# Two transformer stacks on one Trainium2 core: one opening stage, rotations inside the value stages, mixer tables split 8-4-4

## The chip, the core and the metric

The kernel runs on one core of one Trainium2 chip. The metric is the device time of one execution in microseconds (us). Everything is computed in 32-bit floats.

## What is computed

Two blocks follow each other on 512 latent tokens and 256 context tokens of width 1024. The first block has two layers, latent attention (MLA) and gated delta rule (GDN), each with a feed-forward part. The second has windowed attention with a sink and a state-space mixer (S5). Every layer is modulated by a shift, a scale and a gate, which are products of a condition vector with a large matrix. Cut to what the change touches:

```python
mod = silu(c) @ w_mod[i] + b_mod[i]              # 6 x 1024 for the latent tokens, the same with c_ctx for the context
h = x * (1 + scale) + shift
lat = h @ mla_w_in                               # 1024 -> 512 + 256 + 64
cq  = rms_norm(lat[..., :512], q_norm)
ckv = rms_norm(lat[..., 512:768], kv_norm)
k_rope = lat[..., 768:]
q = cq @ w_q_up; kv = ckv @ w_kv_up              # k and v of 8 heads
q_rope, k_rope = rotate(q_rope), rotate(k_rope)  # u1 * cos - u2 * sin, u2 * cos + u1 * sin; latent tokens only
...
abar = exp(lam * dt); bbar = (abar - 1) / lam * b   # S5, complex; the kernel builds tables from their powers
```

## The kernel before, in words

All data is feature-major: 128 features on the partitions, tokens along the free axis. `hu` holds the residual stream h and the modulated input u, both 8 tiles of 768 columns; `area` is a large scratch region; `tmp` and `stat` are small; `P` is the whole of PSUM, four pieces of two banks. `mod` holds the modulation, one column for each row of 128 features and condition.

The program is a sequence of blocks. In a block each engine has its own instruction stream, and a block ends when all engines have come to its end. A wait or a DMA that an engine still has to issue therefore holds everybody.

**Products.** `dense` (line 153) runs one matrix product as a block. The weights come through a ring of two slots: SP loads a slot when TensorE has counted a group in `mm_done` (`stream`, line 136), and prefetches the first two groups of the next product. TensorE does `per` output tiles of `kt` x 128 rows a group over 512 and 256 columns (line 187). In the trace each matmul in 32 bits is two instructions. ScalarE evicts, VectorE works on what was evicted. `dense_tokens` (line 236) does the same with tokens on the partitions, for the values of both attentions: v_up (4 groups, two k tiles) and att_v (2 groups, eight k tiles), six token tiles of 256 columns each.

**Modulation.** One row of `w_mod` (128 x 1024, 512 KB) is multiplied by a condition on VectorE and summed over its columns (`mod_product`, line 1933), twice for each row, as there are two conditions. `mod_stage` (line 1958) does a range of rows beside a `dense`: GpSimd loads them through four slots, VectorE multiplies. `ModStream` does two rows for each group of a `dense`, loaded by SP in the same queue as the weights (line 2001).

**The start**, in this order, each its own block: rows 0 to 15 of the modulation with the loads of x, ctx and constants (lines 2053 to 2092); `s5_prepare`, which computes the powers of the S5 poles in a chain of 32 dependent steps on VectorE with ScalarE's Exp and Sin in between, transposes them on TensorE, and stores three tables (`fa`, `pc`, `a8`) to DRAM, and waits until they have landed (lines 1383 to 1522); `modulate` (line 2115), all 16 passes of u on ScalarE; `dense("mla_in")`, seven output tiles, with rows 16 to 47; a copy; `normalise` for q and for kv (line 278); `dense("q_up")` with rows 48 to 51; a copy of the rotary key; `dense("k_up")`; `dense_tokens("v_up")`; `turn`; attention.

**Rotation.** `turn` (line 343) first loads a permutation and the cosine and sine tables, then for each block of 128 features: TensorE permutes the rows (line 360), VectorE multiplies the permuted block by sin (369) and the block by cos (370), and adds (373). 5 blocks for MLA, 20 for the second attention.

**Mixer tables.** `s5_tables` (line 1525) builds the sixteen S5 tables on GpSimd beside the feed-forward products: 0 to 8 beside ffn_in0, 9 to 13 beside ffn_out0, 14 and 15 beside ffn_in1. It reads `fa` and `pc`; its block can end only when the stores of its last table have landed. The feed-forward blocks ffn_in0 and ffn_in1 also carry a `ModStream` of 44 rows each.

## Time and profile before

| | |
|---|---|
| time, median of 3 runs | 5419.24 us (5417.52 to 5436.85) |
| the profiled execution, its own time | 5445.98 us |
| its span, first to last instruction | 5444.2 us |
| TensorE matmul busy | 4622.4 us, 85% of the span |
| VectorE busy | 1992.6 us, 37% |
| ScalarE busy | 950.8 us, 17% |
| GpSimd busy | 1230.8 us, 23% |
| mean granted TensorE clock | 0.895 |
| HBM | 96 GB/s over the span |

Engines in the rows: PE is TensorE's matmul, PEld its weight load, DVE is VectorE, ACT ScalarE, POOL GpSimd, SP SyncE; a q behind the name is the engine's sequencer, which issues DMAs. `L187` is line 187 of the kernel. A granted clock of 1.00 is 2.4 GHz, 0.50 is 1.2 GHz. Busy shares are means over some forty stages with different limits, so the stages have to be looked at one by one.

### The profile page before, as it was taken

Reading aid. Unit: us, or ns where it says so; the run is one execution under the profiler, and the core shown is the slowest. Engines: PE = TensorE matmul, PEld = TensorE weight load, DVE = VectorE, ACT = ScalarE, POOL = GpSimd, SP = SyncE. Lnnn points to the kernel's source line nnn. Section 1 sums busy time; section 2 is a strip of 40 time slices with the busy share of each in tenths; the row PEclk is TensorE's granted clock in tenths of the full one; section 3 lists DMA queues with packets and bytes.
Section 4 is the critical chain, followed back from the end, with each engine's and each line's share of the span. In section 5 each row is a group of like instructions: output and inputs, shape, how many; then the busy total and the mean of one; then the engine's idle time right before and its main releaser. Section 6 shows DMA issues by size and latency. Waiting matters only on the chain. (4 is left out here: it accounts for less than half of the span.)

```text
span 5444.2 us, 51256 instructions
## 1 busy us (share of the span) xinstructions
PE 4622.4 (85%) x18898; PEld 2798.7 (51%) x18898; DVE 1992.6 (37%) x3915; ACT 950.8 (17%) x2104; POOL 1230.8 (23%) x1460
## 2 busy tenths in 40 slices
PE   2789979998979855788898997986789978698998
PEld 1445545554535544677443443555555546594443
DVE  6613236550045566233107412018830017900001
ACT  1112220000021153343101001003420022010000
POOL 0000029998800048800006100001000000340000
PEclk9887889998989876787999998998999989757999
DMA  4310026764401025322216421110001144663211
GB/s 172 129 40 0 16 78 204 199 199 143 147 31 54 28 96 155 104 70 70 73 70 194 166 99 70 47 50 2 0 23 54 46 137 145 237 185 126 77 70 62
DMA packets 244735, 526.70 MB, mean 97 GB/s; under 512 B 140752, under 2 KB 147408, under 8 KB 214992
## 3 DMA queue, kind: packets, MB, share of 16 engines
q1 hardware_dynamic: 189856, 338.20, 19.0%
q0 software_dynamic: 54416, 185.89, 11.2%
q8 instruction: 104, 1.70, 0.1%
q14 instruction: 71, 0.58, 0.0%
q10 hardware_dynamic: 288, 0.32, 0.0%
HBM read 429.42 MB, written 94.77 MB: 96 GB/s over the span
## 5 line engine op out<-in xcount | busy, mean ns | idle before, releaser
L187 PE MATMUL P<-hu,ring 128*128 128x512 f32 (+1 forms) x4896 | 1741.3, 519 | 141.2 <-PEq L2103 60.2
L187 PEld LDWEIGHTS P<-hu,ring 128*128 128x128 f32 x4896 | 935.8, 191 | 946.5 <-issue 898.8
L187 PE MATMUL P<-area,ring 128*128 128x512 f32 (+1 forms) x3104 | 1165.3, 538 | 74.3 <-PEq L162 36.4
L187 PEld LDWEIGHTS P<-area,ring 128*128 128x128 f32 x3104 | 595.0, 192 | 643.8 <-issue 597.3
L2129 DVE SCALAR_TENSOR_TENSOR hu<-hu,tmp 128x512 f32 (+3 forms) x48 | 47.7, 1001 | 835.9 <-ACT tmp L2123 835.9
L1566 POOL TENSOR_TENSOR area<-area 128x512 f32<-128x512 f32 (+2 forms) x128 | 226.3, 1768 | 10.0
L1544 POOL DMA_DIRECT2D area<-s_fa x64 | 40.7, 635 | 790.0 <-POOLq L289 775.6
L449 PE MATMUL P<-area 128*128 (+3 forms) x480 | 185.8, 497 | 27.1 <-POOL area L431 27.1
L1933 DVE SCALAR_TENSOR_TENSOR area<-area 128x1024 f32<-128x1024 f32 x88 | 191.7, 2178 | 31.0 <-DMA area<-in_w_mod 29.5
L1565 POOL TENSOR_TENSOR area<-area 128x512 f32<-128x512 f32 (+2 forms) x128 | 203.0, 1586 | 0.0
L1564 POOL TENSOR_TENSOR area<-area 128x512 f32<-128x512 f32 (+2 forms) x128 | 193.9, 1515 | 38.2 <-DMA area<-in_s_bn 33.7
L2123 ACT ACTIVATE tmp<-P,mod 128x512 f32<-128x512 f32 x72 | 41.3, 615 | 851.5 <-PE P L187 851.5
L1755 PE MATMUL P<-hu,ring 128*128 128x256 f32 (+1 forms) x512 | 168.2, 492 | 24.9 <-PEq L103 24.9
L2152 DVE TENSOR_TENSOR area<-tmp 128x768 f32<-128x768 f32 (+1 forms) x44 | 66.1, 1501 | 314.1 <-ACT tmp L2136 314.1
L2136 ACT ACTIVATE tmp<-P 128x768 f32<-128x768 f32 (+1 forms) x88 | 57.1, 701 | 691.0 <-PE P L187 691.0
L2165 DVE TENSOR_TENSOR area<-area,tmp 128x512 f32 (+3 forms) x48 | 35.3, 778 | 373.7 <-ACT tmp L2161 373.7
L1933 DVE SCALAR_TENSOR_TENSOR area<-stat,area 128x1024 f32<-128x1024 f32 x88 | 163.8, 1861 | 11.1 <-DMA stat<-in_w_mod 5.2
L1712 POOL DMA_DIRECT2D area<-s_b x16 | 8.5, 530 | 694.0 <-POOLq L103 461.0
L472 PE MATMUL P<-tmp,area 128*128 128x128 f32 x1152 | 158.6, 282 | 0.2
L2312 DVE TENSOR_TENSOR area<-area,tmp 128x512 f32 (+1 forms) x16 | 11.1, 692 | 392.8 <-ACT tmp L2309 392.8
L369 DVE TENSOR_TENSOR tmp<-P,area 128x512 f32<-128x512 f32 x25 | 17.1, 684 | 355.6 <-PE P L360 355.6
L1970 POOL DMA_DIRECT2D tmp<-in_w_mod x30 | 15.9, 532 | 579.1 <-POOLq L2103 483.9
(306 smaller groups left out, 5618.8 us busy)
## 6 DMA issues: line engine op xcount, KB each, us to landing
ring<-in_w_ffn_in SPq DMA_DIRECT2D x44, 1024.0 KB, 5.9
ring<-s_c POOLq DMA_DIRECT2D x32, 1152.0 KB, 6.3
area<-in_w_mod SPq DMA_DIRECT2D x52, 512.0 KB, 3.6
stat<-in_w_mod SPq DMA_DIRECT2D x44, 512.0 KB, 3.6
ring<-in_w_ffn_out SPq DMA_DIRECT2D x16, 1408.0 KB, 6.2
s_c<-area POOLq DMA_DIRECT2D x32, 576.0 KB, 3.6
area<-s_fa POOLq DMA_DIRECT2D x64, 256.0 KB, 7.6
area<-in_s_bn POOLq DMA_DIRECT2D x64, 256.0 KB, 8.0
```

The source lines that it names most:

```text
L187: last = nc.tensor.matmul(c.P[:, 2 * s + j, a:b], c.ring[:, slot, (j * kt + k) * 128:(j * kt + k + 1) * 128], x[:, k, a:b], start=k == 0, ...
L449: last = nc.tensor.matmul(S[n % 2][:, a:b], qs[:, j, t * 128:t * 128 + 128], k(i, j, key, key + b - a), start=True, stop=rope is None)
L472: last = nc.tensor.matmul(O[n % 2], vs[:, j, key, :], probT[:, n % 2, b * 128:b * 128 + 128], start=b == 0, stop=b == len(tiles) - 1)
L1564: tt(out, re_, a, ALU.mult)
L1565: step(tt(tmp, im_, b, ALU.mult))
L1566: step(tt(out, out, tmp, ALU.add if sign > 0 else ALU.subtract))
L1755: last = nc.tensor.matmul(c.P[:, 2 * (g % 2) + j, a:b], c.ring[:, s, (j * KD + k) * 128:(j * KD + k + 1) * 128], c.u[:, k, a:b], start=k = ...
L1933: return c.nc.vector.scalar_tensor_tensor(out=junk, in0=weights, scalar=1.0, in1=c.view(CONDS, 2, D)[:, cc % 2, :], op0=ALU.mult, op1=ALU. ...
L2123: last = act_fn(tmp[:, a:b], ps[:, a:b], ACT.Copy, scale=c.mod[:, bass.ds(g * per + (j + gate), 1), cc:cc + 1].rearrange("p a b -> p (a b)"))
L2129: return vec_fn.scalar_tensor_tensor(out=hk, in0=hk, scalar=ALPHA, in1=tmp[:, 0:w].unsqueeze(1), op0=ALU.mult, op1=ALU.add)
L2136: return act_fn(tmp[:, 0:w], ps[:, 0:w], ACT.Silu if j == 0 else ACT.Copy)
L2152: return vec_fn.tensor_tensor(hidden[:, one(g), 0:w], pairs_first[0][:, 0:w].unsqueeze(1), tmp[:, 0:w].unsqueeze(1), ALU.mult)
```

## The change

One block, `opening`, takes the place of the modulation of rows 0 to 15, `s5_prepare`, `modulate`, `dense("mla_in")`, the copy and both norms. SP and GpSimd load modulation rows and x and ctx tile by tile. VectorE makes the four products of one k and adds the bias, ScalarE makes tile k of u, and TensorE multiplies it with the weights of the first four output tiles, which are all loaded before and accumulate in the four pieces of PSUM. Tiles 4 to 6 follow, then sums of squares, transposes. VectorE does the chain of the powers when the modulation is done, and the scalings by the norms last; the root is Ln and Exp instead of Sqrt and reciprocal. The tables are stored without a wait; the wait stands at the end of SP's stream in q_up (`settle`).

Rows 16 to 35 of the modulation move to q_up, 36 to 43 to k_up, 44 to 51 to a `ModStream` in mla_out, which also loads and activates the conditions; ffn_in0 then does not. The rotary key is evicted straight to its place, so the copy block behind q_up goes. The rotations become part of `dense_tokens`: TensorE permutes between value tiles and, where blocks are left, behind them; GpSimd multiplies by cos, VectorE by sin and adds. The mixer tables are split 8, 4 and 4.

```diff
@@ program @@
-    s5_prepare(c)
-    modulate(modulated(0))
...
-    early = mod_stage(c, "mla_in", 16, 48, mod_slots, flat_stat[:, 0:D])
-    dense(c, "mla_in", u, BOTH, copy_to(lat, per=1), pool=early[0], vector=early[1])
...
-    normalise(c, "q_rms", lat, 4, T, BOTH, 1e-6, vcol("mla_q_norm"))
-    normalise(c, "kv_rms", lat[:, 4:6, :], 2, T, BOTH, 1e-6, vcol("mla_kv_norm"))
...
-    late = mod_stage(c, "q_up", 48, 52, mod_slots, flat_stat[:, 0:D])
+    opening(c, lat, q_all[:, 0, :])
+    early = mod_stage(c, "q_up", 16, 36, mod_slots, flat_stat[:, 0:D])
     dense(c, "q_up", lat, BOTH, lambda g, j, ps, tmp: act_fn(q_all[:, one(g * 2 + (j + 1)), :], ps[:, 0:T].unsqueeze(1), ACT.Copy),
-          pool=late[0], vector=late[1])
-    with nc.Block() as block:
...
-            act_fn(q_all[:, 0, :], k_hold, ACT.Copy)
-    dense(c, "k_up", lat[:, 4:6, :], BOTH, copy_to(k_nope))
-    dense_tokens(c, "v_up", lat[:, 4:6, :], 256, v_tok)
-    turn(c, "mla_rope", q_all, 5, area(13 * T, 3, 512), ("mla_trig", "mla_perm"))
+          pool=early[0], vector=early[1], settle=lambda sp: sp.wait_ge(c.s5_stored, 48))
+    late = mod_stage(c, "k_up", 36, 44, mod_slots, flat_stat[:, 0:D])
+    dense(c, "k_up", lat[:, 4:6, :], BOTH, copy_to(k_nope), pool=late[0], vector=late[1])
+    dense_tokens(c, "v_up", lat[:, 4:6, :], 256, v_tok, (q_all, 5, area(13 * T, 3, 512), ("mla_trig", "mla_perm")))
...
-    residual("mla_out", q_all[:, 5:13, :], 16, (0, 1), BOTH)
+    residual("mla_out", q_all[:, 5:13, :], 16, (0, 1), BOTH, mods=ModStream(c, "mla_out", 44, 4, fresh=0))
...
-                 (lambda pool: s5_tables(c, pool, KF * T, 0, 9), lambda pool: s5_tables(c, pool, KF * T, 9, 14)),
-                 mods=ModStream(c, "ffn_in0", 52, KF, fresh=0))
+                 (lambda pool: s5_tables(c, pool, KF * T, 0, 8), lambda pool: s5_tables(c, pool, KF * T, 8, 12)),
+                 mods=ModStream(c, "ffn_in0", 52, KF))
...
-    feed_forward(1, (0,), LATS, hidden, (lambda pool: s5_tables(c, pool, KF * T, 14, 16), None),
+    feed_forward(1, (0,), LATS, hidden, (lambda pool: s5_tables(c, pool, KF * T, 12, 16), None),
...
-    dense_tokens(c, "att_v", u, 256, v2)
-    turn(c, "att_rope", qk, 20, area(24 * T, 3, 512), ("att_trig", "att_perm"))
+    dense_tokens(c, "att_v", u, 256, v2, (qk, 20, area(24 * T, 3, 512), ("att_trig", "att_perm")))
@@ dense_tokens @@
+    per = blocks // groups
         @block.sync
         def _(sp):
-            stream(c, sp, name, ahead)
+            sp.dma_start(perm, c.ins[tabs[1]]).then_inc(landed, 16)
+            sp.dma_start(tables[:, 0:2, :].rearrange("p a b -> p (a b)"), c.ins[tabs[0]]).then_inc(landed, 16)
+            stream(c, sp, name)
         @block.tensor
+            def partners(n):
+                if n >= 2:
+                    pe.wait_ge(turned, n - 1)
+                nc.tensor.matmul(spare[n % 2], perm, y[:, n, 0:LAT], start=True, stop=True).then_inc(partner, 1)
+            pe.wait_ge(landed, 32)
+            for g in range(groups):
...
                 for t in range(T // 128):
+                    if t % 2 == 0 or per > 3:
+                        if n < blocks and n < (g + 1) * (per + 1):
+                            partners(n)
+                            n += 1
...
+            while n < blocks:
+                partners(n)
+                n += 1
+        @block.gpsimd
+            for n in range(blocks):
+                pool.wait_ge(partner, n + 1)
+                nc.gpsimd.tensor_tensor(y[:, n, 0:LAT], y[:, n, 0:LAT], cos, ALU.mult).then_inc(kept, 1)
+        @block.vector
+            for n in range(blocks):
+                dve.wait_ge(partner, n + 1)
+                if n >= 2:
+                    dve.wait_ge(done, n - 1)
+                nc.vector.tensor_tensor(c.tmp[:, n % 2, 0, 0:LAT], spare[n % 2], sin, ALU.mult).then_inc(turned, 1)
+                dve.wait_ge(turned, n + 1)
+                dve.wait_ge(kept, n + 1)
+                nc.vector.tensor_tensor(y[:, n, 0:LAT], y[:, n, 0:LAT], c.tmp[:, n % 2, 0, 0:LAT], ALU.add).then_inc(done, 1)
@@ new: opening @@
+        @block.sync
+            sp.dma_start(flat(conds), ins["conds"][0:1, :].broadcast_to([128, 2 * D])).then_inc(conds_in, 16)
+            sp.dma_start(first_w[0], ins["w_mod"][0]).then_inc(mod_in[0], 16)
+            sp.dma_start(h[:, 0, 0:LAT], x[:, 0, :]).then_inc(x_in[0], 16)
+            for n in range(0, 4, 2):
+                sp.dma_start(weights[n], ins["w_mla_in"][n]).then_inc(w_in[n], 16)
+            for k in range(1, KD):
+                sp.dma_start(first_w[k], ins["w_mod"][k]).then_inc(mod_in[k], 16)
+                sp.dma_start(h[:, k, 0:LAT], x[:, k, :]).then_inc(x_in[k], 16)
...
+            sp.wait_ge(mm, 4)
+            c.load_slot(sp, "q_up", 0, c.first["q_up"] % 2)
+            c.load_slot(sp, "q_up", 1, (c.first["q_up"] + 1) % 2)
+            sp.wait_ge(turned_k, 4)
+            sp.dma_start(c.s5["fa"].rearrange("r t x y -> x (r t) y"), turned).then_inc(stored, 16)
+            sp.wait_ge(dv, 32)
+            sp.dma_start(c.s5["pc"].rearrange("b p x -> p b x"), pcs).then_inc(stored, 16)
+            sp.dma_start(c.s5["a8"], a8.rearrange("p a b c d -> p (a b c d)")).then_inc(stored, 16)
+        @block.gpsimd
+            for k in range(KD):
+                pool.dma_start(first_w[8 + k], ins["w_mod"][8 + k]).then_inc(mod_in[8 + k], 16)
+                pool.dma_start(h[:, k, LAT:T], x[:, k, :]).then_inc(ctx_in[k], 16)
+                if k == 0:
+                    for n in range(1, 4, 2):
+                        pool.dma_start(weights[n], ins["w_mla_in"][n]).then_inc(w_in[n], 16)
+            nc.gpsimd.memset(eps, 1e-6).then_inc(based, 1)
...
+        @block.tensor
+            for n in range(4):
+                pe.wait_ge(w_in[n], 16)
+            for k in range(KD):
+                pe.wait_ge(shifted, k + 1)
+                for j in range(4):
+                    for a, b in BOTH:
+                        last = mmul(c.P[:, j, a:b], weights[j][:, 128 * k:128 * k + 128], u[:, k, a:b], start=k == 0, stop=k == KD - 1)
...
+            tile(4)
+            pe.wait_ge(consts, 32)
+            pe.wait_ge(kept, 4)
+            sums(range(4), c.P[:, 3, :])
+            tile(5)
+            tile(6)
+            pe.wait_ge(kept, 5)
+            sums(range(4, 6), c.P[:, 0, :])
+            pe.wait_ge(dv, 28)
+            pe.wait_ge(kept, 6)
+            for n in range(4):
+                if n >= 2:
+                    pe.wait_ge(turned_k, n - 1)
+                for m in range(4 * n, 4 * n + 4):
+                    last = nc.tensor.transpose(c.P[:, 1, 512 * (n % 2) + 128 * (m % 4):512 * (n % 2) + 128 * (m % 4) + 128],
+                                               fsel[:, m // 2, m % 2, :], c.ident[:, :])
+        @block.scalar
+            act_fn(flat(conds), flat(conds), ACT.Silu).then_inc(silu_c, 1)
+            for k in range(KD):
+                act.wait_ge(added, k + 1)
...
+                for cc, (a, b) in enumerate(((0, LAT), (LAT, T))):
+                    last = act_fn(u[:, k, a:b], h[:, k, a:b], ACT.Identity, scale=c.mod[:, 8 + k, cc:cc + 1], bias=c.mod[:, k, cc:cc + 1])
...
+            for n in range(4):
+                keep(n)
+            for n in range(4):
+                square(n)
+            act.wait_ge(dv, 14)
+            act_fn(flat(fs), flat(ph), ACT.Sin, scale=TURN)
+            act_fn(flat(fc), flat(fc), ACT.Sin, scale=TURN).then_inc(ac, 1)
+            keep(4)
+            keep(5)
+            square(4)
+            square(5)
+            keep(6)
+            act.wait_ge(based, 3)
+            root(0, c.P[:, 3, :], 512)
+            root(1, c.P[:, 0, :], 256)
+            for n in range(4):
+                act.wait_ge(pe_done, n + 1)
+                act_fn(flat(turned[:, 4 * n:4 * n + 4, :]), c.P[:, 1, 512 * (n % 2):512 * (n % 2) + 512], ACT.Copy).then_inc(turned_k, 1)
+        @block.vector
+            for k in range(KD):
+                for n in (k, 8 + k):
+                    dve.wait_ge(mod_in[n], 16)
+                    for cc in range(2):
+                        if count:
+                            dve.wait_ge(made, count)
+                        mod_product(c, n, cc, first_w[n], junk).then_inc(made, 1)
+                        count += 1
+                if k == 0:
+                    dve.wait_ge(based, 3)
+                dve.wait_ge(made, count)
+                V.tensor_tensor(pair(k), pair(k), base.rearrange("p (a k) -> p a k", a=2)[:, :, k].unsqueeze(2).broadcast_to([128, 2, 2]),
+                                ALU.add).then_inc(added, 1)
...
+            dve.wait_ge(added, KD)
+            dve.wait_ge(ac, 1)
+            step_(tt(grow, re, step, ALU.mult))
...
+            scaled(range(4), 0, "mla_q_norm")
+            scaled(range(4, 6), 1, "mla_kv_norm")
```

## Rows read from the trace of the kernel before

**Rows 1.** Windows of the stages up to q_up, columns by the heading.
```profile
core 0: us, PE busy (x) PEld busy (x) DVE busy (x) ACT busy (x) POOL busy (x), PEclk, DMA share, GB/s
0.00:52.70 52.70, 0.00 (x0) 0.00 (x0) 39.82 (x66) 3.19 (x2) 5.53 (x13) 1.00 0.70 266
52.70:98.90 46.20, 3.68 (x16) 3.27 (x16) 30.46 (x67) 9.38 (x18) 0.00 (x0) 0.92 0.20 61
98.90:108.90 10.00, 0.00 (x0) 0.03 (x1) 0.00 (x0) 9.68 (x16) 0.00 (x0) 0.50 0.00 0
108.90:184.50 75.60, 75.51 (x224) 43.52 (x224) 66.59 (x108) 4.92 (x7) 15.91 (x30) 0.96 0.72 247
184.50:198.50 14.00, 0.00 (x0) 0.00 (x0) 12.74 (x22) 0.76 (x1) 1.06 (x2) 0.58 0.35 131
198.50:235.60 37.10, 11.52 (x24) 5.96 (x24) 20.85 (x13) 7.81 (x9) 0.00 (x0) 0.64 0.00 0
235.60:300.80 65.20, 64.96 (x192) 37.48 (x192) 10.03 (x17) 7.59 (x11) 2.10 (x4) 0.96 0.20 69
```
**Rows 2.** Timeline of the first stage: start us, us, engine, line, operation.
```profile
6.40 17.71 SPq L2060 DMA_DIRECT2D ones<-in_ones  x1
9.83 1.23 DVE L1933 SCALAR_TENSOR_TENSOR stat<-area 128x1024 f32<-128x1024 f32 x1 [9.83 <-DMA area<-in_w_mod]
```
**Rows 3.** Groups of VectorE's instructions by line, 0 to 53 us.
```profile
L1933 DVE SCALAR_TENSOR_TENSOR stat<-area 128x1024 f32<-128x1024 f32 x32 | 39.2, 1225 | 12.4 <-DMA area<-in_w_mod 9.8 <-DVE stat L1933 0.5
```
**Rows 4.** Window of the DMA in the first stage.
```profile
10.00:15.00 5.00, 0.00 (x0) 0.00 (x0) 4.76 (x8) 0.00 (x0) 0.00 (x0) 1.00 1.03 417
```
**Rows 5.** Window of TensorE's clock at mla_in's start.
```profile
109.00:115.00 6.00, 6.00 (x7) 2.38 (x8) 1.25 (x3) 0.00 (x0) 2.11 (x4) 0.50 0.72 235
```
**Rows 6.** Timeline of the mixer powers: first step, transposes, last copy, last store.
```profile
55.55 0.29 DVE L1450 TENSOR_TENSOR area<-area 128x128 f32<-128x128 f32 x1 [3.21 <-ACT area L1425]
...
84.05 3.68 PE L1521 MATMUL P<-ident,area 128*128 128x128 f32 x16 [84.05 <-DVE area L1497]
...
87.76 0.60 ACT L1435 ACTIVATE area<-P 128x512 f32<-128x512 f32 x1 [0.26 <-PE P L1521]
...
90.46 3.70 SPq L1419 DMA_DIRECT2D s_a<-area  x1
```
**Rows 7.** Timeline of both value stages and their rotations.
```profile
329.34 20.96 PE L257 MATMUL P<-ring,area 128*128 128x256 f32 x96 [1.86 <-PEq L162]
...
352.43 0.43 SPq L352 DMA_DIRECT2D area<-in_mla_perm  x1
356.82 6.50 PE L360 MATMUL P<-area 128*128 128x512 f32 x10 [6.51 <-DMA area<-in_mla_perm]
...
368.38 0.69 DVE L373 TENSOR_TENSOR area<-area,tmp 128x512 f32<-128x512 f32 x1
...
3601.05 41.68 PE L257 MATMUL P<-ring,hu 128*128 128x256 f32 x192 [1.97 <-PEq L162]
...
3691.06 0.69 DVE L373 TENSOR_TENSOR area<-area,tmp 128x512 f32<-128x512 f32 x1
```
**Rows 8.** Windows behind ffn_in0 and ffn_out0, and of ffn_in1 with tables beside it.
```profile
1229.10:1252.80 23.70, 0.01 (x1) 0.00 (x0) 8.28 (x4) 1.51 (x2) 14.25 (x14) 0.54 0.39 141
1482.90:1491.50 8.60, 0.03 (x2) 0.05 (x1) 0.96 (x1) 1.05 (x2) 0.00 (x0) 0.75 0.43 152
2878.60:2991.50 112.90, 111.72 (x255) 49.23 (x256) 82.59 (x71) 10.74 (x16) 91.86 (x66) 0.98 0.77 228
```
**Rows 9.** Timeline of GpSimd: tables' first and last DMA in ffn_in0, two products.
```profile
772.86 0.63 POOL L1544 DMA_DIRECT2D area<-s_fa  x1 [202.76 <-POOLq L289]
...
1244.08 0.60 POOL L1601 DMA_DIRECT2D s_fb<-area  x1 [0.30 <-POOL area L1566]
...
1261.70 1.26 POOL L1564 TENSOR_TENSOR area<-area 128x512 f32<-128x512 f32 x1 [4.34 <-DMA area<-in_s_bn]
...
2986.24 2.13 POOL L1564 TENSOR_TENSOR area<-area 128x512 f32<-128x512 f32 x1
```

More of the change, by code:

```diff
@@ L55 @@
 PRODUCTS = [
-    ("mla_in", 8, 1), ("q_up", 4, 2), ("k_up", 2, 2), ("v_up", 2, 2), ("mla_out", 8, 2),
+    ("q_up", 4, 2), ("k_up", 2, 2), ("v_up", 2, 2), ("mla_out", 8, 2),
     ("ffn_in0", 8, 2), ("ffn_out0", KF, 1),
@@ L165, in _ @@
             stream(c, sp, name, more=mods and mods.load)
+            if settle:
+                settle(sp)
         if pool:
@@ L233, in _, with dense_tokens @@
                 vector(eng)
-def dense_tokens(c, name, x, width, out, ahead=True):
+def dense_tokens(c, name, x, width, out, turn):
     nc = c.nc
@@ L240, in dense_tokens @@
     at, groups = c.first[name], c.ins["w_" + name].shape[0]
-    copied = c.sem(name + "_copied")
+    copied, landed, partner, turned, kept, done = (c.sem(f"{name}_{n}") for n in ("copied", "landed", "partner", "turned", "kept", "turn_done"))
     psum = c.P[:, :, :].rearrange("p a b -> p (a b)")
+    y, blocks, tables, tabs = turn
+    cos, sin, perm = tables[:, 0, :], tables[:, 1, :], tables[:, 2, 0:128]
+    spare = [psum[:, 1536:2048], psum[:, 3584:4096]]
+    per = blocks // groups
     with nc.Block() as block:
```

415 lines of the change are left out of this document (191 added, 224 removed).

## The prediction

> **What bounds the kernel now.** I read the windows by stage first, because the change reshapes a few stages out of some forty and the rest keeps its length. Up to 108.9 us TensorE does nothing but 16 transposes: 52.7 us of modulation products on VectorE, 46.2 us of mixer powers with their stores, 10.0 us in which ScalarE alone modulates. Then mla_in holds TensorE for 75.6 us, 14.0 us pass in which VectorE finishes 64 modulation products, and the two norms take 37.1 us with TensorE busy in 11.5 of them. q_up's first matmul starts at 235.6 us [rows 1]. The reader should see that the engines take turns: before q_up the work that only TensorE can do (75.5 us of mla_in and 11.5 us of sums) is little over a third of the time. Two more places are serial: each rotation stands behind its value stage [rows 7], and in ffn_in0 GpSimd, which builds 9 of 16 mixer tables there, is done 15 us after TensorE, so that TensorE idles 23.7 us; at the end of ffn_out0 a tail of the same kind makes 8.6 us [rows 8, 9].
>
> **The opening.** VectorE starts its first product at 9.83 us, when modulation row 0 has landed [rows 2]; 32 products took 39.2 us busy at 1225 ns [rows 3], and from 9.83 to 52.7 about 1.31 us each with the read-out and the wait. The four products of a pair k take 5.2 us; the new add after each pair I take at 0.3 us, so 5.5 us a pair. DMA: before VectorE can start k=1, some 5.7 MB must land (condition rows 1, rows 0 and 8 together 1, rows 1 and 9 together 1, x and ctx of k=0 0.4, four weight tiles 2, vectors 0.3); at 417 GB/s [rows 4] from about 3 us on that is 17 us, against 15.3 when VectorE is free. I charge 1.7 us, once: a later pair needs 1.4 MB, 3.3 us, less than VectorE's 5.5. VectorE ends at 17 + 7 x 5.5 = 55.5, say 56; ScalarE's pair of passes (9.68 us for eight pairs [rows 1], 1.2 each) ends the last tile at 57.5.
>
> TensorE works beside this. Seven tiles of mla_in took 75.5 us [rows 1]; the first 6.0 us, after an idle stretch, ran at a granted clock of 0.50, 1.2 GHz [rows 5], which costs 3 us; so 10.35 us a tile. Four tiles for one k are an eighth of four, 5.2 us, against 5.5 us between tiles of u, so TensorE follows VectorE: it starts at 17, has made up the slow start by the third k, and ends k=7 at 62.7. Then, in its program's order: tile 4 (73), four sums of squares (5.2, to 78.2), tiles 5 and 6 (to 99), two sums (to 101.5). ScalarE's squares lie inside tile 4. The powers' chain runs on VectorE beside it: 55.55 to 84.05 before [rows 6], now from 59 plus some 3 us for the sines that queue behind ScalarE's squares, to about 91. It is hidden with 10 us to spare; if it came that much later it would show one for one. Behind the last sum comes what is exposed: two Ln and Exp pairs, and 16 transposes with four copies that took 3.7 us before (84.05 to 87.76 [rows 6]), together to about 109. ScalarE does them in order, so the copies stand behind the roots. VectorE's six scalings (0.9 us each, 1225 ns scaled to 768 columns) are over by then. SP issues the stores of the tables behind the last copy; their issue alone took from 88.4, when the last copy was done, to 94.16, the third blocked for 3.70 us [rows 6]: 5.8 us, and an engine that issues holds the stage open. End 115. The landing wait (until 98.9 before) moves to q_up's end, where it is long over. q_up starts at 115 instead of 235.6: **-120.6 us**.
>
> Unknowns of the opening. ScalarE's two roots may need one load of its function tables or several: I give this 3 us down and 4 up, between 112 and 119. GpSimd issues 18 DMAs before it makes the base of the sums for which VectorE waits at k=0; at about 0.55 us each this ends at 11 us, free. If GpSimd's queue blocked as SP's did, whose eleventh issue took 17.71 us [rows 2], VectorE would stand until about 24: up to +10 us. I take zero, since the nearest rows of GpSimd's own queue, the eight loads and ctx, show no such wait.
>
> **Products moved.** 32 rows leave mla_in. q_up takes 20: 40 x 1.31 + 4.4 to the first landing + 0.7 = 57.5 us, under its 65.2 [rows 1]; if the stores delay the loads by 5 us it still fits. k_up takes 8: 16 x 1.31 + 5.1 = 26.1 us, which passes its 20.7 us of warm matmul, so VectorE ends that stage; since the copy block ahead of it goes (1.2 us) and the stage had lasted 25.6, from q_up's end to v_up's start comes **-0.5 us**. mla_out takes 8 beside 82 us of matmul, with the conditions' DMA and Silu ahead of ScalarE's first eviction, which is due after 20 us: +0.2 us for a last small add. ffn_in0 loses its reload of the conditions, which hid.
>
> **v_up and its rotation.** Before: 329.3 to 369.1 [rows 7]. Now TensorE waits first for the tables, which SP can only issue at the stage's start: 4.8 us by the same pair of DMAs (the second issue at 352.43, the first 0.4 before it, the partner matmul at 356.82). TensorE then is cold, 3 us. 21.0 of values, five partner products of 0.86: 4.3. Last copy 1.5. End 329.3 + 34.7: **-5 us**.
>
> **att_v and its rotation.** Before: 3601.05 to 3691.7 [rows 7], of which 40 us are 20 turns of 2.0 us. Now 5 + 3 + 41.7 + 12 partners (10.3) bring it to 3661; eight turns are left behind the values. VectorE's share of a turn falls from three passes of 0.6 to two, 1.4 us with the dependence. But GpSimd's product takes 1.26 us alone [rows 9], and beside VectorE's two-input work 2.13 [rows 9]. If the two exclude each other in the add, a turn is 1.26 + 0.69 = 2.0 us, no shorter than before; if not, 1.4. I take 2.0, by the row with both at work: 16 us, plus 1.5, to 3678.7: **-13 us** (at 1.4: -18; at 2.8: -7).
>
> The Trainium skill, "SBUF — State Buffer", section "Who interferes with whom", says that a VectorE instruction with two SBUF inputs and a GpSimd instruction that reads SBUF block each other for a whole instruction. By it the turn is 2.0 us and the move of the cosine product to GpSimd buys nothing in the tail. The trace agrees as far as it goes: products of 1.23 us on VectorE stretch beside the tables (82.6 us busy in 112.9 [rows 8]).
>
> **Tables.** GpSimd took 471 us for 9, from 772.86 to 1244.1 [rows 9]: 52.4 each. Eight end at 1192, before TensorE's end at 1229; what then ends ffn_in0 is ScalarE's eviction, VectorE's product and three small adds, about 3.6 us: 23.7 - 3.6 = **-20.1 us**. In ffn_out0, four instead of five end 50 us early; 8.6 us become about 4.2, an eviction of two ScalarE passes, VectorE's residual and the change of blocks, an estimate from the 3.6 above: **-4.4 us**. In ffn_in1 four instead of two: with GpSimd at work 1.2 us of TensorE were lost in 112.9 [rows 8]; I take as much again: **+1.2 us**. Four end after 260 of 306 us.
>
> **Sum.** -120.6 - 0.5 - 5 + 0.2 - 13 - 20.1 - 4.4 + 1.2 = -162. The profiled execution took 5445.98 us, 27 above the median of the runs shown. Against itself it would be 5284; taken off the median, 5419 - 162 = **5257 us**.
>
> **Rivals.** (1) *The forecast*, chance 0.72: 5235 to 5280.
> (2) *TensorE stays at 1.2 GHz while it is fed tile by tile.* A k then takes 10.3 us, eight take 82, and the phase ends at 99 instead of 62.7: +37, or with GpSimd's blocked queue +10: 5267 to 5304. For it: TensorE waits before each k, and after gaps of some us it runs slow [rows 5]. Against: at half clock it is behind VectorE and so never idle, which is how it got its clock back in 6 us in mla_in. Chance 0.14.
> (3) *More is won*: turns of 1.4 us, warm starts, stores issued faster: 5235 and below, down to 5228. Chance 0.08.
> (4) *The change doesn't pay in its side parts*: rotations bring nothing, ffn_in0 is held by its two-condition products. Only the opening: 5419 - 121 = 5298. Chance 0.04.
> (5) *Slower than before.* In ffn_in1 SP loads each weight slot behind the wait for the modulation products of the group before. If four tables lock VectorE so that four products and the silu product take more than TensorE's 14 us a group (111.7 us for eight [rows 8]), every group waits. To lose the 162 us over 22 groups a group would have to take 21 us; at 27 (products of 6 us, five times their 1225 ns) it is 22 x 13 = +286, less the 162: 5543. For it: VectorE's work per group is already 10 us there, not 6. Against: TensorE idled for 1.2 us in those eight groups. Chance 0.02.
>
> **How the numbers follow.** The range 5230 to 5302 takes in (1), (2) and most of (4); what it leaves out is the far end of (3), (5), and the 19 us by which the runs of before differ. About 0.5%, 27 us, is what a measurement of this kernel can tell from no change. Faster by more: 0.96, all of (1) to (4) but 0.02 kept for something unseen that eats the gain, which is the chance of no change; slower: 0.02, (5).
>
> **What would show it.** q_up's first matmul near 115 us; matmuls of the opening from 17 us, granted clock 1.00 from about 23; k_up ended by VectorE; TensorE of both value stages starting 5 us late; eight turns of 2.0 us behind att_v; ffn_in0's gap 3 to 4 us; GpSimd over by 3150 in ffn_in1. Wrong if q_up starts after 130, if TensorE in ffn_in1 idles over 5 us, or if stages that the change doesn't touch change by over 10 us in sum.

## The result and the profile after

The changed kernel takes **5267.31 us** (median of 4 runs, 5254.79 to 5272.83) against 5418.38 us for the kernel before beside it (4 runs, 5412.9 to 5436.85): ratio 0.97, interval 0.968 to 0.9719, 151 us less, inside the range 5230 to 5302. Its profiled execution took 5272.83 us with a span of 5271.1, and is 5.5 above its median; that of before was 27 above its own, so between the two traces lie 173 us.

The page of the changed kernel: busy time by engine, and TensorE's busy tenths and granted clock in 40 slices of 132 us:

```profile
PE 4601.1 (87%) x18898; PEld 2791.0 (53%) x18898; DVE 1979.2 (38%) x3891; ACT 954.4 (18%) x2108; POOL 1274.8 (24%) x1489
...
PE   7899799999799656888989997977799788798998
...
PEclk9878899999899766888999998999999999658999
```

TensorE's busy tenths before, in slices of 136 us, were

```profile
PE   2789979998979855788898997986789978698998
```

The first digits are what changed: TensorE is busy for seven tenths of the first slice instead of two. The windows of the opening stages, after (columns as in [rows 1]):

```profile
core 0: us, PE busy (x) PEld busy (x) DVE busy (x) ACT busy (x) POOL busy (x), PEclk, DMA share, GB/s
0.00:17.50 17.50, 0.00 (x0) 0.00 (x0) 5.09 (x9) 4.50 (x4) 11.60 (x25) 1.00 0.88 340
17.50:63.10 45.60, 44.95 (x128) 25.22 (x129) 38.50 (x80) 13.97 (x28) 0.00 (x0) 1.00 0.62 239
63.10:101.90 38.80, 38.80 (x122) 22.82 (x122) 27.14 (x51) 13.27 (x17) 0.00 (x0) 1.00 0.08 28
101.90:118.60 16.70, 2.94 (x18) 2.33 (x16) 5.75 (x6) 9.18 (x11) 0.00 (x0) 0.61 0.32 95
118.60:184.70 66.10, 64.14 (x193) 37.19 (x193) 49.70 (x82) 9.07 (x12) 10.66 (x20) 0.97 0.64 214
184.70:210.50 25.80, 20.86 (x64) 12.03 (x64) 20.08 (x34) 6.04 (x8) 4.21 (x8) 0.95 0.59 205
210.50:245.90 35.40, 26.90 (x106) 20.93 (x106) 6.92 (x10) 5.81 (x4) 8.76 (x9) 0.89 0.29 92
```

TensorE waits for its first data until 17.5 us, then is full for 84.4 us in two windows, with VectorE and ScalarE at work beside it, and idles again for most of the 16.7 us ahead of q_up. What stood one behind the other in [rows 1] now lies side by side. The stages, from each one's first matmul to the next one's, in the two traces:

```
                             before   after    difference   forecast
start to q_up                 235.6    118.6     -117.0      -120.6
q_up, k_up, v_up with turns   136.2    127.3       -8.9        -5.5
MLA attention                 263.0    261.6       -1.4         0
mla_out                        87.0     87.3       +0.3        +0.2
ffn_in0                       480.4    460.5      -19.9       -20.1
ffn_out0                      238.6    232.5       -6.1        -4.4
norm behind it                 53.5     48.6       -4.9         0
delta-rule heads              681.2    677.7       -3.5         0
ffn_in1                       309.1    307.7       -1.4        +1.2
att_qk and att_v              304.0    288.5      -15.5       -13
second attention              306.1    309.6       +3.5         0
```

The rows with a forecast and the norm make -173 (forecast -162); all stages that no edit touches make less than 1 us in sum in this pair of traces, though single ones move by 3.5.

### The profile page after: what moved, and what is told of

Read it like the earlier page. It is cut to its first block and busy times, and to the rows that moved or that the text cites. A ratio compares the mean times of both kernels' runs of the same rounds, so it can differ in the third digit from the quotient of the medians.

```text
span 5271.1 us, 51177 instructions
## 1 busy us (share of the span) xinstructions
PE 4601.1 (87%) x18898; PEld 2791.0 (53%) x18898; DVE 1979.2 (38%) x3891; ACT 954.4 (18%) x2108; POOL 1274.8 (24%) x1489
## 5 line engine op out<-in xcount | busy, mean ns | idle before, releaser
L189 PE MATMUL P<-hu,ring 128*128 128x512 f32 (+1 forms) x4672 | 1665.9, 520 | 118.7 <-PEq L333 40.1
L189 PEld LDWEIGHTS P<-hu,ring 128*128 128x128 f32 x4672 | 892.4, 191 | 892.0 <-issue 849.2
L1802 DVE SCALAR_TENSOR_TENSOR area<-stat,area 128x1024 f32<-128x1024 f32 x96 | 207.1, 2157 | 8.0 <-DMA stat<-in_w_mod 1.7
L1624 PE MATMUL P<-hu,ring 128*128 128x256 f32 (+1 forms) x512 | 168.3, 492 | 24.9 <-PEq L103 24.9
L1624 PEld LDWEIGHTS P<-hu,ring 128*128 128x128 f32 x512 | 98.1, 192 | 94.8 <-issue 88.1
L483 PEld LDWEIGHTS P<-tmp,area 128*128 128x128 f32 x1152 | 144.7, 197 | 1.9 <-ACT tmp L518 1.7
```

What stands on the lines that cost most here:

```text
L189: last = nc.tensor.matmul(c.P[:, 2 * s + j, a:b], c.ring[:, slot, (j * kt + k) * 128:(j * kt + k + 1) * 128], x[:, k, a:b], start=k == 0, ...
L483: last = nc.tensor.matmul(O[n % 2], vs[:, j, key, :], probT[:, n % 2, b * 128:b * 128 + 128], start=b == 0, stop=b == len(tiles) - 1)
L1624: last = nc.tensor.matmul(c.P[:, 2 * (g % 2) + j, a:b], c.ring[:, s, (j * KD + k) * 128:(j * KD + k + 1) * 128], c.u[:, k, a:b], start=k = ...
L1802: return c.nc.vector.scalar_tensor_tensor(out=junk, in0=weights, scalar=1.0, in1=c.view(CONDS, 2, D)[:, cc % 2, :], op0=ALU.mult, op1=ALU. ...
```

## The experiments

**The base again.** After all others the changed kernel was timed once more, beside the last two versions.

> The changed kernel unaltered, beside the two others on the same chip and with the same runs of before, so that their difference from it can be read: 5255 to 5273, as before. Stages that no edit touches (MLA attention, the delta-rule heads, the second attention) will again lie several us apart from those of its first trace; the opening, ffn_in0, ffn_out0 and att_v will not (within 0.6 us).

Measured: 5251.25 us (5236.21 to 5254.81), ratio 0.9677 (0.9653 to 0.9701), 172 us under the 5423.25 of before; so it lay a few us under the interval that I gave. MLA attention 250.7 instead of 261.6, heads 667.7 instead of 677.7, ffn_in0 460.7, ffn_out0 232.7, att_v 72.9, q_up at 117.98 instead of 118.60. The same program did the same work in other time. In the stages of the table above that the edits touch, and the norm, this second trace is 172.8 us under the one of before (the first 173.2); in all other stages together it is 23.9 under it, where the first was 0.1 above. The windows from 440 to 480 us, inside MLA attention, first the changed kernel's first trace:

```profile
440.00:480.00 40.00, 37.17 (x132) 19.08 (x131) 11.26 (x31) 9.00 (x19) 3.91 (x5) 0.74 0.00 0
```

and the second:

```profile
440.00:480.00 40.00, 37.17 (x165) 20.25 (x163) 14.72 (x39) 11.09 (x24) 3.91 (x5) 1.00 0.00 0
```

TensorE is busy for 37.17 of 40 us in both, at a granted clock of 0.74 and of 1.00, and gets through 132 and 165 matmuls. Over the whole of MLA attention TensorE is idle for 9.3 us in both traces and busy for 252.3 and 241.4, at granted clocks of 0.80 and 0.84: the 10.9 us are the clock's. So a part worth under 10 us can't be told from a total; below, each part is read in its own stage and the total only bounds it.

**The tables split 9-5-2 again**, all else as in the changed kernel (lines cut):

```
-  s5_tables(c, pool, KF * T, 0, 8), ... s5_tables(c, pool, KF * T, 8, 12)
+  s5_tables(c, pool, KF * T, 0, 9), ... s5_tables(c, pool, KF * T, 9, 14)
-  s5_tables(c, pool, KF * T, 12, 16)
+  s5_tables(c, pool, KF * T, 14, 16)
```

> The changed kernel with the mixer tables split 9-5-2 again. My theory: GpSimd outlasts TensorE in ffn_in0 and ffn_out0 and nothing else depends on the split. Then the gap behind ffn_in0 is some 24 us instead of 3.7, the gap behind ffn_out0 some 8 us instead of 2.6, and TensorE comes cold to the sums of the norm behind it (13.5 and 12.3 us instead of 10.6 and 10.6): +30 us, about 5297. ffn_in1 stays at 305 us of TensorE. Rival A, the gaps alone, clock untouched: +25. Rival B, two more tables beside ffn_in1 cost TensorE time there: ffn_in1 gets 2 us or more shorter when they go, and the sum is under +25.

Measured: 5284.31 us (5280.22 to 5286.1), ratio 0.9736 (0.9692 to 0.978): 17 above the changed kernel's first median and 33 above its second. By stage +20.6 in ffn_in0, +6.5 in ffn_out0, +4.5 in the norm behind it: 31.6, as my theory had it. In the totals of the two traces MLA attention, which ran 10.9 us shorter in this one, hides a third of that. TensorE's timeline of this kernel at ffn_out0's start and at the two halves of the norm's sums:

```profile
1114.63 6.08 PE L189 MATMUL P<-area,ring 128*128 128x512 f32 x7 [24.04 <-PEq L162]
...
1353.64 13.36 PE L339 MATMUL P<-hu,ones 128*128 128x512 f32 x32 [8.90 <-PEq L162]
1368.93 12.28 PE L344 MATMUL P<-tmp,ones 128*128 128x512 f32 x32 [1.93 <-ACT tmp L354]
```

and the changed kernel's:

```profile
1107.06 229.94 PE L189 MATMUL P<-area,ring 128*128 128x512 f32 x704 [3.67 <-PEq L162]
...
1339.60 10.56 PE L339 MATMUL P<-hu,ones 128*128 128x512 f32 x32 [2.61 <-PEq L162]
1352.09 10.59 PE L344 MATMUL P<-tmp,ones 128*128 128x512 f32 x32 [1.93 <-ACT tmp L354]
```

The gaps fall from 24.04 to 3.67 and from 8.90 to 2.61. The same 64 matmuls behind the second gap take 25.6 us after 8.90 us of idleness, at granted clocks of 0.79 and 0.86 in the two halves, and 21.2 us after 2.61, at 1.00 in both: behind the shorter gap TensorE kept its clock. ffn_in1, which has two tables here and four in the changed kernel, takes 307.6 here and 307.7 there: four cost nothing.

**The rotations behind their stages again** (the loop over blocks in a stage of its own, as before; all else as changed):

```
-    dense_tokens(c, "att_v", u, 256, v2, (qk, 20, area(24 * T, 3, 512), ("att_trig", "att_perm")))
+    dense_tokens(c, "att_v", u, 256, v2)
+    turn(c, "att_rope", qk, 20, area(24 * T, 3, 512), ("att_trig", "att_perm"))
```

> The changed kernel with the value stages and the rotations as separate blocks again, as in the kernel before. My theory: the traces' differences of 6.7 us (v_up) and 15 us (att_v) are the rotations' own: +22 us, about 5289. Rival, the value stages' cold start and the wait for the tables eat most of it: +10 or less.

Measured: 5282.74 us (5272.73 to 5299.82), ratio 0.9735 (0.9685 to 0.9785). att_qk and att_v together 303.4 instead of 288.5, +14.9; MLA attention starts 136.3 us behind q_up's first matmul (255.73 less 119.40) instead of 127.3, +9.0. In sum +23.9, against my +22; the rival (+10 or less) is out. As in the kernel before, VectorE does the cosine product here too; the next run shows that this adds nothing.

**The cosine product on VectorE** instead of GpSimd:

```
+                nc.vector.tensor_tensor(y[:, n, 0:LAT], y[:, n, 0:LAT], cos, ALU.mult).then_inc(kept, 1)
-        @block.gpsimd
...
-                nc.gpsimd.tensor_tensor(y[:, n, 0:LAT], y[:, n, 0:LAT], cos, ALU.mult).then_inc(kept, 1)
```

> The changed kernel with the product by cos on VectorE instead of GpSimd, inside the same stages. My theory (GpSimd's product and VectorE's add exclude each other, 1.27 + 0.69 us): the eight turns behind att_v take 2.0 us each either way, so the stage's length changes by under 1 us and the time stays within 3 us. Rival, the move to GpSimd takes work off the path: a turn gets 0.6 us longer, 5 us in the tail.

Measured: 5263.43 us (5226.44 to 5272.03), ratio 0.9679 (0.9621 to 0.9737); att_v 72.7 instead of 72.8. A turn in this kernel's tail, timeline:

```profile
3503.08 0.68 DVE L303 TENSOR_TENSOR tmp<-P,area 128x512 f32<-128x512 f32 x1
3503.68 0.68 DVE L304 TENSOR_TENSOR area<-area 128x512 f32<-128x512 f32 x1
...
3504.47 0.69 DVE L307 TENSOR_TENSOR area<-area,tmp 128x512 f32<-128x512 f32 x1
3505.07 0.68 DVE L303 TENSOR_TENSOR tmp<-P,area 128x512 f32<-128x512 f32 x1
```

and three turns of the changed kernel's:

```profile
3497.91 4.17 POOL L302 TENSOR_TENSOR area<-area 128x512 f32<-128x512 f32 x3 [3.04 <-PE P L265]
3499.29 1.67 DVE L314 TENSOR_TENSOR area<-area,tmp 128x512 f32<-128x512 f32 x1 [0.73 <-POOL area L302]
3500.88 0.68 DVE L311 TENSOR_TENSOR tmp<-P,area 128x512 f32<-128x512 f32 x1
3501.59 1.04 DVE L314 TENSOR_TENSOR area<-area,tmp 128x512 f32<-128x512 f32 x1
```

Three passes on VectorE come to 1.99 us a turn (3503.08 to 3505.07). With the cosine on GpSimd VectorE has two, but its add (L314, both inputs in SBUF) takes 1.67 and 1.04 us instead of 0.69 while GpSimd multiplies, and GpSimd's three products 4.17 instead of 3 x 1.27; the product that reads PSUM (L311) keeps its 0.68. Eight such turns end no sooner than eight on VectorE alone (17.0 us from the tail's first product to its last add with GpSimd, 17.1 without). The Trainium skill, "SBUF — State Buffer", section "Who interferes with whom", has this rule: a VectorE instruction with two SBUF inputs and a GpSimd one that reads SBUF exclude each other, one with a single SBUF input, outside its 2-port performance modes, does not. The trace agrees on both halves, and the run shows what follows: this part of the change is worth 0.

**Only the side parts**: the kernel before with the fused rotations and the split 8-4-4, without the new opening (against the kernel before, shortened; att_v is changed as v_up is).

```
-    dense_tokens(c, "v_up", lat[:, 4:6, :], 256, v_tok)
-    turn(c, "mla_rope", q_all, 5, area(13 * T, 3, 512), ("mla_trig", "mla_perm"))
+    dense_tokens(c, "v_up", lat[:, 4:6, :], 256, v_tok, (q_all, 5, area(13 * T, 3, 512), ("mla_trig", "mla_perm")))
...
-  0, 9 and 9, 14 and 14, 16
+  0, 8 and 8, 12 and 12, 16
```

> The kernel before with only the rotations inside the value stages and the tables split 8-4-4; the opening is the old one. My theory, the parts add up: v_up 6.7, att_v 15, behind ffn_in0 19.9, behind ffn_out0 6.1, warm norm 4.8, together -52 us, about 5366, and so 100 to 120 us for the opening. Rival, the parts depend on each other (the modulation of rows 44 to 51 in mla_out shortens something in ffn_in0, the opening's gain is larger alone): the sum is off by 10 us or more.

Measured: 5369.21 us (5358.47 to 5377.42), ratio 0.9895 (0.9848 to 0.9943): 50 us of gain against 5419.22, and q_up still at 235.61. By stage its trace gives 53.4 in the stages touched, where I had expected 52. With the opening's 117.0 that makes 170.4 of the 173.2 by which these stages shrank in the changed kernel: the parts add up. The opening was not run alone; its 117 are the difference that is left.

**The two roots in the order Ln, Ln, Exp, Exp:**

```
-            root(0, c.P[:, 3, :], 512)
-            root(1, c.P[:, 0, :], 256)
+            log(0, c.P[:, 3, :], 512)
+            log(1, c.P[:, 0, :], 256)
+            root(0)
+            root(1)
```

> The two roots of the opening in the order Ln, Ln, Exp, Exp instead of Ln, Exp, Ln, Exp; nothing else. Theory: each change between the two functions loads a table for 1.28 us, four of them between 100.28 and 108.15, and these lie on the path (copies of the transposes, last store, q_up). Two loads go (2 x 1.28), the last root ends at about 106.4 instead of 108.99, the stores are issued 2.5 us earlier, and q_up's first product starts at about 116.1 instead of 118.60. Rival: the last transposes or the powers' stores set the end anyway (those stores are issued from 112.60 because of the queue, not of the copies): q_up stays at 118 or later. In the total -2.5 us at most, which three rounds can't tell; it is read from the trace.

In the changed kernel ScalarE's timeline from the last sums of squares to the copies of the transposes reads:

```profile
100.28 1.28 ACT L2078 ACT_TABLE_LOAD   x1
...
102.49 1.28 ACT L2080 ACT_TABLE_LOAD   x1
...
104.65 1.28 ACT L2078 ACT_TABLE_LOAD   x1
...
106.86 1.28 ACT L2080 ACT_TABLE_LOAD   x1
108.15 0.84 ACT L2080 ACTIVATE hu<-hu 128x768 f32<-128x768 f32 x1
108.90 1.07 ACT L2098 ACTIVATE area<-P 128x512 f32<-128x512 f32 x2
```

and with the roots paired:

```profile
100.22 1.28 ACT L2078 ACT_TABLE_LOAD   x1
101.52 1.69 ACT L2078 ACTIVATE hu<-P,area 128x768 f32<-128x768 f32 x2
...
103.23 1.28 ACT L2083 ACT_TABLE_LOAD   x1
104.52 1.58 ACT L2083 ACTIVATE hu<-hu 128x768 f32<-128x768 f32 x2
```

Two loads for four, and q_up's first matmul at 115.53 instead of 118.60, 3.1 us earlier: two loads of 1.28 us and some overlap of like operations. Total 5257.9 us (5241.64 to 5265.76), ratio 0.97 (0.9653 to 0.9747), not to be told from the changed kernel's, as expected.

**The stores waited for in the opening:**

```
             sp.dma_start(c.s5["a8"], a8.rearrange("p a b c d -> p (a b c d)")).then_inc(stored, 16)
+            sp.wait_ge(stored, 48)
```

> Inside the opening stage SyncE waits for the three mixer stores before the stage ends, instead of leaving the wait to the end of q_up. Theory: the last store lands some 2 to 4 us behind its issue (114.45 to 118.15), and this goes on the path in full: q_up's first product at about 122 to 123 instead of 118.60, so moving the wait is worth 4 to 5 us, and the total is 4 us longer, inside what runs can tell. Rival: the stores have landed by the time that the issue queue lets SyncE go (its 3.70 us of issue is itself the wait for room), then q_up starts within 1.5 us of 118.60. The modulation loads in q_up no longer queue behind the stores: their first product comes nearer to the stage's start than the 6.9 us of the changed kernel.

Measured: q_up's first matmul at 122.09, and as the opening's tile 4 began 0.64 us earlier here (62.49 against 63.13), the wait costs 4.1 us. This part of the change is worth that. It has a small price: with the stores still under way the first modulation product of q_up starts 6.9 us behind q_up's first matmul (125.48 less 118.60), here 4.25 (126.34 less 122.09); q_up hides both. Total 5249.89 us (5242.77 to 5259.1), ratio 0.9693 (0.965 to 0.9737).

**The rotation tables issued in the stage before**, first at that stage's end (settle), then at its head:

```
-            sp.dma_start(perm, ...) and sp.dma_start(tables, ...)        in v_up and att_v
+    dense(c, "att_qk", ..., settle=turn_tables(c, *att_tabs, att_in))    e_tables_early
+    dense(c, "att_qk", ..., head=turn_tables(c, *att_tabs, att_in))      e_tables_first
```

> The rotation tables of both value stages are issued by SyncE at the end of the stage before (k_up, att_qk) and not at the start of the value stage. Theory: the first product of each value stage waits for SyncE's two table issues and the weights behind them (v_up's at 214.82 and att_v's at 3442.87 with 9.26 and 6.61 us idle before them). With the tables gone from the queue's head both start about 4 to 5 us earlier and TensorE stays at full clock, so that the stages end 5 to 7 us earlier each: v_up through to MLA attention 245.92 to about 240, att_v stage 72.8 to about 67; total -10 to -13 us. Rival: the stage start itself (barrier, semaphores, first weight tile over DMA) is the wait, and the tables lie beside it: less than 2 us each, total within 4 us of the changed kernel.

Measured: 5252.78 us (5248.39 to 5256.48), ratio 0.969 (0.9648 to 0.9733), and by stage almost nothing: att_v 73.0, MLA attention at 245.72. SyncE's and TensorE's timeline at att_v tells why:

```profile
3423.83 0.34 SPq L120 DMA_DIRECT2D ring<-in_w_att_v  x1
...
3424.21 0.44 SPq L317 DMA_DIRECT2D area<-in_att_perm  x1
3424.69 0.43 SPq L318 DMA_DIRECT2D area<-in_att_trig  x1
3430.22 2.07 PE L263 MATMUL P<-area 128*128 128x512 f32 x2 [6.42 <-DMA area<-in_att_trig]
```

In att_qk the last weight load waits for room in the ring until the last group is done, and the tables stand behind it in SyncE's program, so that att_v had them as late as before, and this run tests neither theory there. In k_up they were issued at 208.12 instead of 210.54, and v_up's first product came at 213.21 instead of 214.82; v_up then took 1.4 us longer, for a reason that I did not find. At the head of the stage, with SyncE's and TensorE's rows at the same place:

> The rotation tables of both value stages are issued as SyncE's first two instructions of the stage before (k_up, att_qk), ahead of the weights that wait for room in the ring; in the run before this one they stood behind those weights, were issued only as that stage ended, and the first product of att_v waited for them still (6.42 us, ended by the tables' DMA). Theory: the tables' transfer is the wait, and its place ahead of the blocked issues takes it away. att_v's first product waits about 2 us, as k_up's does (1.96 us behind the stage before), instead of 6.61, and TensorE keeps the full clock, so that the first 4 rotation and value products take half as long too: att_v 72.8 to 66 to 68 us. v_up's first product comes at 211.5 to 212.5 instead of 214.82 and gains 1 to 3 us, because TensorE has waited there for VectorE's last modulation products already and starts at the low clock either way. Total -6 to -9 us against the changed kernel, inside what the medians tell; it is read by stage. Rival: the stage's start (barrier and first weights) is the wait, then att_v stays above 71 us.

```profile
3380.67 20.98 SPq L120 DMA_DIRECT2D ring<-in_w_att_v  x2
3403.39 1.10 PE L265 MATMUL P<-area 128*128 128x512 f32 x2 [2.12 <-PEq L162]
```

att_v's first product now waits 2.12 us instead of 6.61 and runs at full clock, 1.10 us for the pair instead of 2.08. att_qk is 4.4 us shorter (211.0 against 215.4; the wait counts there) and att_v 2.7 (70.3 against 72.9). v_up's first product comes at 211.89 instead of 214.82 and MLA attention starts at 243.92, 2.0 earlier. In sum 9 us; the total, 5233.61 us (5227.17 to 5258.25), ratio 0.9658 (0.9631 to 0.9686), is 18 under the changed kernel beside it. Its trace is 22 under that kernel's, of which the heads, 9.4 us shorter with no edit in them, are chance.

**The opening with tile 6 last**, behind the transposes and both sums, with the stores and the second root beside it (TensorE's part of the edit; ScalarE's program follows it, with the first root beside tile 5):

```
             tile(5)
-            tile(6)
...
+            pe.wait_ge(dv, 28)
+            turns(0, 2)
             pe.wait_ge(kept, 5)
             sums(range(4, 6), c.P[:, 0, :])
...
+            turns(2, 4)
+            pe.wait_ge(kept, 6)
+            tile(6)
```

> The opening in another order: TensorE makes tile 6 (the rotary key) last, behind the sums of squares and the transposes, so that both roots with their four table loads, the copies and the stores run on ScalarE, VectorE and the queues beside tile 6's 32 products. Nothing is left out. Theory: the 19.35 us between TensorE's last product of the changed kernel's opening (99.25) and q_up's first (118.60) is a chain of ScalarE, transposes and issues that needs no TensorE; beside tile 6 (about 10.5 us) most of it is hidden: q_up's first product at 106 to 108 instead of 118.60, total -10 to -12 us. Rival: the stores of the mixer tables are late by the powers' chain on VectorE (last at 91.85) and SyncE's issues (112.16 to 118.15), so that the end moves by less than 5 us; or the waits put on TensorE ahead of tile 6 cost it its clock and tile 6 takes 21 us instead of 10.5, and q_up starts at about 117.

Measured: 5235.17 us (5230.78 to 5244.67), ratio 0.9666 (0.9623 to 0.971). Its timeline from the last transposes to q_up:

```profile
92.90 10.49 PE L2015 MATMUL P<-hu,tmp 128*128 128x512 f32 x32
...
93.77 0.39 SPq L1977 DMA_DIRECT2D s_fa<-area  x1
94.21 1.82 SPq L1979 DMA_DIRECT2D s_pc<-area  x1
...
95.98 1.28 ACT L2084 ACT_TABLE_LOAD   x1
96.07 3.68 SPq L1980 DMA_DIRECT2D s_a<-area  x1
...
104.54 35.71 PE L189 MATMUL P<-area,ring 128*128 128x512 f32 x109 [1.15 <-PEq L1957]
```

The stores with their 3.68 us of issue, the second root and its tables stand inside tile 6's 10.49 us, in which the granted clock is 1.00, and q_up follows 1.15 us behind it instead of 7.09. It starts at 104.54: 14.1 us earlier, 1.5 beyond the expected 106.

**Both together:**

> The opening with tile 6 last and the rotation tables issued first, together. Theory: both act in stages apart and add up: q_up's first product at 104.5 as with the opening's order alone, MLA attention about 15 to 17 us earlier than in the changed kernel's 245.92 (229 to 231), att_v about 5 us shorter; total 18 to 22 us below the changed kernel: about 5240 by the medians of earlier runs, ratio to before 0.965 to 0.967. Rival: with q_up earlier the modulation products in q_up and k_up become the bound (they run beside it on VectorE and waited for loads), and half of the opening's gain is given back: MLA attention at 238 or later.

Measured: **5226.4 us** (5206.35 to 5234.82, 5 runs), ratio 0.9632 (0.9609 to 0.9654). Its slowest run is below the fastest of the changed kernel beside it (5236.21), and the medians lie 24.9 apart. The stages touched give the same: MLA attention starts at 228.23 instead of 246.22, and att_qk with att_v takes 282.0 instead of 288.4, 24.4 in sum. The rival (MLA attention at 238 or later) is out. In one point I was off: q_up began at 105.80 and not at 104.5. Here TensorE was done with the first tile of u earlier, idled for 1.96 us (0.60 in the changed kernel) and then lost its clock for a few products, as the window behind that gap shows:

```profile
26.10:30.00 3.90, 3.88 (x8) 2.11 (x9) 3.73 (x8) 0.03 (x1) 0.00 (x0) 0.64 1.03 394
```

The 112 products behind it took 38.08 us instead of 36.76. This version beats both kernels.

## Why the prediction was right, point by point

**The likeliest case came.** The forecast's steps gave -162 and the two traces give -173 in the same stages. The second timing of the changed kernel gave -172, the first -151; the forecast lies between. How near the first median came is luck in part. By stage the sum was 11 us short, 3.6 too much for the opening and 14.6 too little for the rest, and the stages that no edit touches, which I had put at nothing, lie between 0.1 us above and 36.9 below those of before over the twelve later traces. My sign of being wrong, over 10 us of change in those stages, is no test for the same reason: two traces of one program give 0.1 and -23.9.

**The opening** was 3.6 us too short. Its first half held by two errors that cancel: VectorE waited for pair k=1 until 19.83 and not 17, as its timeline shows,

```profile
19.83 1.23 DVE L1802 SCALAR_TENSOR_TENSOR stat<-area 128x1024 f32<-128x1024 f32 x1 [4.29 <-DMA area<-in_w_mod]
```

but a pair then took 5.23 us, not 5.5, so that the last add ended at 56.3, where I had 56. The windows (340 GB/s over 17.5 us, then 397) have 6.9 MB moved by 19.83, where I had counted 5.7: about 1.2 MB that this pair did not need had come with it. Which, no run tried. TensorE started at 17.55 and ended the last k at 63.1, where I had 62.7. The second half is where the term was mis-sized. The "two Ln and Exp pairs, and 16 transposes with four copies ... together to about 109" ended at 112.14. From 101.5 to 109 they had 7.5 us, of which the four passes of the roots (0.90, 0.84, 0.90, 0.84) and the transposes and copies (3.7) fill 7.2, so there was room for none of ScalarE's four table loads of 1.28 us; with two of them gone q_up started at 115.53. The stores' issue took 6.0 us (112.16 to 118.15), where I had 5.8 from [rows 6]. My bounds, 112 to 119, held it. The chain of the powers on VectorE ended at 92.07 and was hidden, as forecast.

**Rival 2, TensorE at 1.2 GHz while fed tile by tile**, is out by TensorE's timeline:

```profile
17.55 8.38 PE L2005 MATMUL P<-hu,ring 128*128 128x512 f32 x16 [17.55 <-DMA ring<-in_w_mla_in]
...
26.53 36.76 PE L2005 MATMUL P<-hu,ring 128*128 128x512 f32 x112 [0.60 <-ACT hu L2054]
```

The next 112 matmuls went through in 36.76 us, 0.33 each, without a gap. The slow start that I had charged came, though: the first 16 took 8.38 us, 3.1 more than 16 at 0.33. The window says a granted clock of 1.00 there, but TensorE's weight loads (PEld) say otherwise. Their rows in the opening, and behind them those of q_up's start, where the granted clock is given as 0.50:

```profile
21.09 0.34 PEld L2005 LDWEIGHTS P<-hu,ring 128*128 128x128 f32 x1 [0.52 <-issue]
23.62 0.19 PEld L2005 LDWEIGHTS P<-hu,ring 128*128 128x128 f32 x1 [0.48 <-issue]
119.58 0.33 PEld L189 LDWEIGHTS P<-area,ring 128*128 128x128 f32 x1 [0.52 <-issue]
122.78 0.19 PEld L189 LDWEIGHTS P<-area,ring 128*128 128x128 f32 x1 [0.30 <-issue]
118.60:122.50 3.90, 3.90 (x5) 1.80 (x6) 0.00 (x0) 0.00 (x0) 2.18 (x4) 0.50 0.97 279
```

A load takes 0.34 us up to 23.6 us and 0.19 from then on, as at q_up when the granted clock goes from 0.50 to 1.00. So TensorE ran its first 6 us at 1.2 GHz; the column's 1.00, which stands there from 0 us on, before TensorE had worked at all, proves nothing. The reason that I gave against the rival held: the slow start kept TensorE on the first tile of u until 0.60 us before the second was ready, and so never idle for long. It lay inside the wait for VectorE and cost nothing at the end. The run with both changes shows the rival's mechanism in small: behind 1.96 us of idleness there the clock fell once more, for 1.3 us of loss. GpSimd's queue did not block either: its last issue of the context was at 10.47 us, 0.61 us long, and the base of the sums was ready for k=0 (GpSimd's last pass on it began at 11.51, the first add at 15.38).

**The products moved** ran as forecast: q_up hid its 40, and VectorE ended k_up (its last add at 209.90, the last matmul at 205.6). With the rotations apart, q_up's first matmul to MLA attention's takes 136.3 us, against 136.2 before: the products moved cost 0.2, where I had -0.5.

**The rotations.** The eight turns left behind att_v were there, at 2.0 us, by the row with both engines at work [rows 9]; the run with the rotations apart gives them 14.9 us at att_v and 9.0 at v_up, where I had 13 and 5. At v_up two terms were too large: the slow start after the tables cost 1.8 us (2.08 for 1.02 in the first pair of products, 2.60 for 1.89 in the eight behind it), not the 3 that I charged; and I counted the wait for the tables from v_up's first matmul (329.34), which itself stood 1.86 us behind k_up's last. The 5 us of late tables that I charged to each stage were real, and the run with the tables at the head takes most of them out.

**The tables.** The gap behind ffn_in0 came to 3.67 us (I had 3.6) and that behind ffn_out0 to 2.61, where I had 4.2. What the sum lacked altogether is the clock of what follows: the norm's sums ran at a granted clock of 1.00 and not 0.78 and 0.86, -4.9 us. In ffn_in1 I charged 1.2 us for four tables; it gained 1.4, and TensorE ran through in one piece, in its timeline:

```profile
2718.75 304.73 PE L189 MATMUL P<-hu,ring 128*128 128x512 f32 x704 [15.89 <-PEq L333]
```

So **rival 5** is out in this kernel. Of the 1.4 us, 1.19 are a stall on a weight load that stood in the kernel before and not here. It does not go by the number of tables: with two the stage had this stall before and none in the run 9-5-2, with four none in the changed kernel and two, of 1.1 and 0.7 us, in the run with the side parts alone. Its cause stays open; it is far from the 7 us a group that the rival needed. **Rival 4** is out by the same run (50 us won in the side parts), and **rival 3**, a time of 5235 or less, by both medians; turns of 1.4 us did not come, though the norm at full clock is one of the warm starts that it named.

## What to carry to other kernels

Read what one stage keeps waiting by its end, not its sum: the new opening won by putting four engines' work side by side, and it left 16.7 us more of the same kind, most of which went when the one piece of TensorE's work that nobody waits for was moved behind the pieces that others wait for. A load that must be early has to be issued ahead of any wait for room in its queue's program; at the end of the stage before it gained nothing. When two gaps of like size close, look one stage on: here idle time shortened from 8.9 to 2.6 us gave back another 4.5 in TensorE's clock. And add up the stages touched and the stages untouched apart: over two traces of one program the first agree within 0.5 us, the second differ by 24.

## What had not been expected of the hardware

ScalarE loads a table of 1.28 us at each change between Ln and Exp at this place: four loads for Ln, Exp, Ln, Exp and two for Ln, Ln, Exp, Exp. The Trainium skill, "ScalarE activation tables: per-element evaluation and per-set limits", section "What a function is on this engine", says that two functions of different sets are one such load (1283 ns) apart. The trace agrees with the figure.

The time of stages that no edit touches varies: MLA attention took 250.7 to 265.0 us over the traces, the heads 654 to 681. In MLA attention it is the clock, as shown (0.74 or 1.00 in the same 40 us); in which executions it comes back early was not settled. In the heads it is not TensorE's clock: in the two traces of the changed kernel TensorE was busy for 493.0 and 493.5 us, at 0.76 in both, and the 9.9 us are waits, whose cause is open. Two medians of 4 runs of that one program lie 16 us, 0.3%, apart.
